# An encoder trunk on eight cores: feed-forward sums and products on VectorE alone, and a down projection one token block at a time

## The reference

```python
def swiglu(x, w_gate, w_up, w_down):
    return (jax.nn.silu(x @ w_gate) * (x @ w_up)) @ w_down
...
        h = swiglu(rms_norm(x, g[0]), ffn_w_gate[l, 0], ffn_w_up[l, 0], ffn_w_down[l, 0])
        x = x + HALF * rms_norm(h, g[1])
```

## Time and profile before

| | us |
|---|---|
| median of the 3 runs (2834.23, 2855.17, 2928.75) | 2855.17 |
| the profiled execution | 2832.33 |
| its slowest core, first to last instruction | 2830.8 |
| spans of its eight cores | 2819.8 to 2830.8 |
| PE busy on the slowest core | 2567.1 (91%) |
| DVE busy | 1661.7 (59%) |
| ACT busy | 1284.7 (45%) |
| POOL busy | 1160.9 (41%) |

### The profile page before, as it was taken

One profiled execution on the slowest core, in us unless ns is written; L12 is line 12 of the kernel. 1 busy time (PEld: TensorE's weight loads), 2 busy tenths in 40 slices (PEclk: granted clock), 3 DMA queues, 4 the chain that ended last, 5 costly groups with the idle time before them and its releaser, 6 DMA issues.

```text
span 2830.8 us, 39197 instructions; the slowest of 8 cores (2819.8 to 2830.8 us)
## 1 busy us (share of the span) xinstructions
PE 2567.1 (91%) x11634; PEld 1142.2 (40%) x11634; DVE 1661.7 (59%) x2166; ACT 1284.7 (45%) x2160; POOL 1160.9 (41%) x1337
## 2 busy tenths in 40 slices
PE   6899699988999799879969987997999996998997
PEld 2344244433454344334424433442445442443442
DVE  4752963455375964486197458616555669635643
ACT  5442443537777543344255344423117674433532
POOL 2742772115220674367167346710002106734751
PEclk8999899999999899989989999998999998999999
DMA  8455754748560355475475447553235504546767
GB/s 183 69 92 88 169 82 70 136 81 140 73 107 1 97 75 81 71 172 86 72 172 84 74 83 164 88 73 79 45 53 84 88 1 104 83 76 122 146 102 152
DMA packets 140349, 270.29 MB, mean 95 GB/s; under 512 B 16496, under 2 KB 35184, under 8 KB 140144
## 3 DMA queue, kind: packets, MB, share of 16 engines
q0 software_dynamic: 108432, 189.02, 44.6%
q1 hardware_dynamic: 31712, 78.77, 9.0%
HBM read 417.90 MB, written 34.60 MB: 160 GB/s over the span
## 4 chain that ended last, share of the span: by engine, by line
PE 76%; DVE 10%; issue 7%; ACT 3%; DMA 2%; POOL 1%; SPq 0%; DVEq 0%; ACTq 0%; POOLq 0%
PE ps L336 76%; DVE X L843 2%; DVE XH L799 2%; DVE X L842 1%; DMA X<-xT 1%; DVE XN L799 1%; DVE FE L1163 0%; DMA slotf_54<-wflat 0%; ACT L746 0%; DVE H L1014 0%; DVE ET_107 L1163 0%; DMA M_151<-memT 0%; DMA slotf_55<-wflat 0%; ACT r_65 L749 0%; POOL SW_0_82 L959 0%
## 5 line engine op out<-in xcount | busy, mean ns | idle before, releaser
L814 ACT ACTIVATE X<-ps,cf_sb 128x512 f32<-128x512 f32 x128 | 87.9, 687 | 429.5 <-PE ps L336 429.5
L336 PE MATMUL ps<-XH,SW_2_84 128*128 128x512 f16 x344 | 101.2, 422 | 69.4 <-DVE ER_88 L1000 16.0
L959 POOL TENSOR_TENSOR SW_0_82<-slotf_53 128x512 f16<-128x512 f16 x42 | 52.7, 1255 | 190.7 <-DVE X L843 190.2
L336 PE MATMUL ps<-XN,WQK 128*128 128x512 bf16 x512 | 124.0, 379 | 0.0
L336 PE MATMUL ps<-XH,SW_2_87 128*128 128x512 f16 x344 | 94.7, 400 | 24.5 <-DVE ER_89 L1000 12.8
L336 PE MATMUL ps<-TX_80,SW_1_86 128*128 128x512 f16 x344 | 90.7, 386 | 25.7 <-ACT ps L985 25.1
L985 ACT ACTIVATE ps<-ps 128x512 f32<-128x512 f32 x172 | 100.5, 584 | 28.9 <-PE ps L336 28.0
L843 DVE TENSOR_TENSOR X<-X 128x512 f32<-128x512 f32 x120 | 111.6, 958 | 0.0
L336 PE MATMUL ps<-TX_80,SW_1_83 128*128 128x512 f16 x344 | 92.0, 388 | 19.9 <-ACT ps L985 11.0
L792 ACT ACTIVATE XN<-X 128x512 bf16<-128x512 f32 x160 | 94.9, 628 | 20.0 <-DVE X L843 11.3
L336 PE MATMUL ps<-XH,slotf_52 128*128 128x512 f16 x360 | 96.6, 385 | 7.9 <-DVE XH L799 7.9
(11 more groups left out here) (528 smaller groups left out, 6542.8 us busy)
## 6 DMA issues: line engine op xcount, KB each, us to landing
xscr<-X SPq DMA_DIRECT2D x48, 512.0 KB, 9.1
X<-xscr SPq DMA_DIRECT2D x48, 512.0 KB, 7.6
slotf_52<-wflat POOLq DMA_DIRECT2D x62, 256.0 KB, 4.4
slotf_53<-wflat POOLq DMA_DIRECT2D x62, 256.0 KB, 5.0
slotf_54<-wflat POOLq DMA_DIRECT2D x62, 256.0 KB, 4.8
slotf_55<-wflat POOLq DMA_DIRECT2D x62, 256.0 KB, 5.1
slotf_56<-wflat POOLq DMA_DIRECT2D x62, 256.0 KB, 4.4
slotf_57<-wflat POOLq DMA_DIRECT2D x62, 256.0 KB, 5.4
```

The lines of the kernel that those rows point to most:

```text
L336: self.q["pe"].append((waits, (lambda e: e.matmul(out, lhsT=l_, rhs=r_, start=st, stop=sp, skip_group_check=grp)), inc))
L814: k.later({"act": lambda e: e.activation(out=oap, in_=P[bank][:, :], func=AF.Copy, scale=gcol)}, reads=[("P", bank)] + CONST, writes=okeys ...
L959: fn = lambda e: e.tensor_tensor(out=o_, in0=a, in1=b, op=op)
```

## The change

1. Line 959 (four a tile) and line 1024 (one a tile) may run on DVE alone; POOL is no longer a choice for them.
2. In the FFN, the addition to x in the post-norm (line 843) runs on DVE alone (`spread=False`). After the mixers and the attention it keeps its choice.
3. Every down stage goes one token block at a time: all 8 chunks of the first block, its `finish` (post-norm and, where there is a next sub-layer, the pre-norm of that block), then all 8 chunks of the second block. The panels are loaded for each block, 48 instead of 24 a half in halves 1 to 7. The pre-norm's squares are summed by DVE for the first block of a half and by PE for the second; before, DVE summed both in halves 1, 3, 4 and 5, and PE both in halves 2 and 6. Halves 7 and 8 have no pre-norm: their results are stored to `yT` (line 854).

```diff
--- before.py
+++ after.py
@@ -831,7 +831,7 @@
                     acc_add(sq, acc, sq, ak + sqk, sqk)
                     stat_later(self.st, self.psk, sq, sqk, True, False)
 
-            def apply(self, c):
+            def apply(self, c, spread=True):
                 tb = self.tb
                 lo, hi = tbr(tb)
                 st = self.st
@@ -842,12 +842,12 @@
                 mul = lambda e: e.tensor_tensor(out=hap, in0=hap, in1=R[st["r"]][:, :], op=ALU.mult)
                 add = lambda e: e.tensor_tensor(out=xap, in0=xap, in1=hap, op=ALU.add)
                 k.later({"dve": mul}, reads=hkeys + [self.rk], writes=hkeys, post=self.use, dyn=lambda: ([("R", st["r"])], []))
-                k.later({"dve": add, "pool": add}, reads=hkeys + [xk(c, tb)], writes=[xk(c, tb)])
-
-        def finish(pns, nxt, acc=True, by_chunk=False):
+                k.later({"dve": add, "pool": add} if spread else {"dve": add}, reads=hkeys + [xk(c, tb)], writes=[xk(c, tb)])
+
+        def finish(pns, nxt, acc=True, by_chunk=False, spread=True):
             order = [(pn, c) for c in range(8) for pn in pns] if by_chunk else [(pn, c) for pn in pns for c in range(8)]
             for pn, c in order:
-                pn.apply(c)
+                pn.apply(c, spread)
                 if nxt is None:
                     lo, hi = tbr(pn.tb)
                     yv = yT.rearrange("(c p) t -> p c t", p=128)
@@ -957,7 +957,7 @@
 
                 def ew(o_, a, b, op, rk, wk):
                     fn = lambda e: e.tensor_tensor(out=o_, in0=a, in1=b, op=op)
-                    k.later({"dve": fn, "pool": fn}, reads=rk, writes=wk, cost={"dve": 0.42, "pool": 1.5})
+                    k.later({"dve": fn}, reads=rk, writes=wk, cost={"dve": 0.42})
                 ew(s1, a21, a22, ALU.add, uk, q1)
                 ew(s2, s1, a11, ALU.subtract, q1 + gk, q2)
                 ew(a21, a11, a21, ALU.subtract, gk + uk, uk)
@@ -1022,7 +1022,7 @@
                     k.later({"act": lambda e: e.activation(out=e2, in_=e2, func=AF.Silu)}, reads=q2, writes=q2, func="silu")
                     hap, hkeys = H(j, (TB, 2 * TB))
                     fn = lambda e: e.tensor_tensor(out=hap, in0=e2, in1=e3, op=ALU.mult)
-                    k.later({"dve": fn, "pool": fn}, reads=q2 + q3, writes=hkeys, cost={"dve": 0.7, "pool": 1.4})
+                    k.later({"dve": fn}, reads=q2 + q3, writes=hkeys, cost={"dve": 0.7})
 
         def plain_tile(wg, wu, j, tb):
             lo, hi = tbr(tb)
@@ -1068,29 +1068,11 @@
                     if (l, f) == (0, 0):
                         mem_norm()
                     token_sums(1)
-                if nxt is None and hf == 1:
-                    for tb in tbs:
-                        tl = ((tb % 2) * TB, (tb % 2 + 1) * TB)
-                        pn = PostNorm(l, n_post, tb, True, hoap=ho_x(tb))
-                        for c in range(8):
-                            slots = [ws.acquire(("d", l, f, c, pc)) for pc in range(3)]
-                            b = k.bank()
-                            pairs = []
-                            for j in range(NJ):
-                                rap, rkeys = H(j, tl)
-                                sl = slots[j // 8]
-                                pairs.append((sl.w(j % 8), rap, rkeys + [sl.key]))
-                            k.mm(P[b][:, :], pairs, b)
-                            pn.evac(c, b)
-                            for sl in slots:
-                                ws.release(sl)
-                        finish([pn], nxt)
-                    continue
-                pn = {tb: PostNorm(l, n_post, tb, True, hoap=ho_x(tb)) for tb in tbs}
-                for c in range(8):
-                    slots = [ws.acquire(("d", l, f, c, pc)) for pc in range(3)]
-                    for tb in tbs:
-                        tl = ((tb % 2) * TB, (tb % 2 + 1) * TB)
+                for tb in tbs:
+                    tl = ((tb % 2) * TB, (tb % 2 + 1) * TB)
+                    pn = PostNorm(l, n_post, tb, True, hoap=ho_x(tb))
+                    for c in range(8):
+                        slots = [ws.acquire(("d", l, f, c, pc)) for pc in range(3)]
                         b = k.bank()
                         pairs = []
                         for j in range(NJ):
@@ -1098,12 +1080,13 @@
                             sl = slots[j // 8]
                             pairs.append((sl.w(j % 8), rap, rkeys + [sl.key]))
                         k.mm(P[b][:, :], pairs, b)
-                        pn[tb].evac(c, b)
-                    for sl in slots:
-                        ws.release(sl)
-                finish([pn[tb] for tb in tbs], nxt, hf == 0 or f == 1)
-                for c in range(8):
-                    x_reload(l, f, hf, c)
+                        pn.evac(c, b)
+                        for sl in slots:
+                            ws.release(sl)
+                    finish([pn], nxt, tb % 2 == 0, spread=False)
+                if nxt is not None or hf == 0:
+                    for c in range(8):
+                        x_reload(l, f, hf, c)
 
         def even_mixer(l, n_post, nxt):
             cpk = lambda sg, q: ("CP", sg, q)
```

## The result

The changed kernel takes 2674.74 us (median of 4 runs, 2661.38 to 2706.22), the kernel before beside it 2891.96 (median of 4 runs, 2834.23 to 2961.16). The ratio is **0.9387, with a 95% interval of 0.9249 to 0.9525**: faster. The profiled execution took 2661.38 us (predicted: 2660), its slowest core 2659.8, its cores 2649.5 to 2659.8, so 171 us less than the profiled execution before.

A forecast was written before the change was run, and what follows sets the result against it. PE was taken as the bound, losing time at stage starts behind the norms on DVE and ACT. Terms -119.6 - 14.3 - 32.6 - 15.6 - 4 + 14 = -172 from 2832.3 gave 2660 us; 80% range 2605 to 2735.

The forecast's parts named there:

- After FFN halves: Gate/up stages of halves 2, 4, 5 and 6: excess over the floor falls from 151.6 us together to 8 each, -119.6.
- Half 8: Its gate/up stage, with a post-norm alone ahead: excess falls from 19.3 us to 5, -14.3.
- Odd mixer: The first block's 15.6 us of norm now lie under the down stage: -15.6 us, between -8 and -18.
- Even mixer: In a 50 us stretch of PE's matmuls, 4 of 6.2 us lost are won back.
- After attention: Gate/up stages of halves 3 and 7: norm order unchanged, only prices fall; excess of 64.6 us together halves, -32.6.
- Panels twice: Second panel loads in halves 1 to 7: +4.6 us where half 7's stores join, 1.5 each in halves 1 to 6.
- Middle of a tile: Gate/up tiles: four sums and four result instructions take DVE 4.4 of 6.04 us, so the middle of the stage costs nothing.
- late sums in every tile: Rival: a weight sum reaches PE late in each gate/up tile; 172 tiles cost 34 us, 2694 us; 5%.
- memory-bound down stages: Rival: panels read at twice the rate arrive at 104 GB/s or less, making the kernel slower, 2889 us; 3%.
- late weights: Rival: every down stage waits like the end of half 8 or twice that, 18 to 50 us more, 2678 to 2710; 10%.
- The first rival: Three more sums a tile on an already full DVE cost 11 us a transition, 79 in seven stages: 2739 us; 7%.
- The stretching is not POOL's: Rival: DVE's prices stay as they are and only the halving by token blocks counts: 2742 us; 8%.

The follow-up runs named there:

- pair of reading and writing kernels: Changed kernel plus unused POOL work in each gate/up tile: six additions reading SBUF, 2774.6 to 2779.4 us; or twelve memsets only writing, 2844.71 us (fastest of three).
- the sums alone: Kernel before with line 959, line 1024 and the FFN's line 843 on DVE alone, down stages as before: 0.962 of before, fastest run 2747.40 us.
- `blocks only`: Changed kernel with lines 959, 1024 and 843 allowed on POOL again, down stages still one token block at a time: 0.950 of before, fastest run 2719.24 us.
- half of the memsets: Changed kernel with six unused memsets on POOL in each gate/up tile instead of twelve: 2661.33 and 2662.86 us, 0.935 of before.

## Why the prediction was right

The total, 2660 against 2661.38 for the profiled execution, is right by its main steps. That it is right to 1 us is luck, since errors of up to 10 us cancel in two pairs:

- **After FFN halves** (151.6 to 8 each): 8.2, 8.1, 11.6 and 8.6. Half 5, where four token sums also stand on DVE, is 3.6 over. Of the terms of the 8, DVE's is the better one: at the start of half 4 PE waits 2.1 us for ACT (4 were taken) and 1.7 for DVE (2); the eight matmuls stand at the 1.7 estimated, and some 2.6 us are in no wait of the profile.
- **Half 8** (to 5): 5.9. **Odd mixer** (-15.6): -15.4. **Even mixer** (-4): -4.2 on the slowest core, but some -7 on most of the others (407.6 to 409.4 us on the eight cores before, 399.9 to 404.4 after). **Half 1** (0, up to -10): -4.5, its down stage included, where the eight cores of one execution differ by 7 to 9. It makes up for the 4.5 that the stages after FFN halves won less than forecast.
- **After attention** (-16 each): -11.3 and -11.0. The step that failed is that "the order of the norms is unchanged; only prices fall": the planner gave POOL four additions that had all lain on DVE, and one a stage took 7.67 us behind a busy DVE. With them on DVE it is -15.8 and -14.5. The 149 us named as a sign for these stages was missed by 5.
- **Panels twice** (+14): half 7 +5.5 (+3.8 to +6.2 over the cores) instead of the 4.6 read from the earlier trace rows; halves 2 to 6 0 instead of 1.5 each. Too much here made up for too little after attention.
- **Middle of a tile** (nothing): right. In the changed kernel PE has no wait between 960 and 1043 us.

Of the rivals, late sums in every tile and memory-bound down stages did not come, nor did late weights beyond half 7, which the forecast had. The first rival, DVE as the bound at the transitions, came in small: DVE is without a gap in some 20 us after attention (with line 843 on DVE there), where seven additions fewer gave 1.4 us, and at the start of half 5, the stage that is 3.6 over, PE waits 4.6 us for weight sums. "The stretching is not POOL's" is refuted by the pair of reading and writing kernels, not only by the durations.

One argument was weaker than it looked. The 1.64 and 1.93 us of the earlier trace rows were read where POOL was busy; over the whole kernel before, line 843 of the FFN had a median of 681 ns and a mean of 958, as its rows from two views show, so at least half of its instructions were not stretched at all:

```profile
L843 DVE TENSOR_TENSOR X<-X x120: 674/681/3530, 274.1 to 2826.6; 128x512 f32<-128x512 f32 x120
...
L843 DVE TENSOR_TENSOR X<-X 128x512 f32<-128x512 f32 x120 | 111.6, 958 | 0.0
```

That fits the sums alone bringing 50 us after FFN halves, and not the 72 that I expected of them. The blocks alone bring 89, more than half: the first block's norm goes to a place where POOL has no sums, so that it loses its stretching with its place. The trace of `blocks only` shows that on line 799, first under half 3's down stage (1057 to 1134 us), where POOL only issues transfers, then at the start of half 4 (1134 to 1281 us), where it has sums again:

```profile
L799 DVE SCALAR_TENSOR_TENSOR XH<-X,cf_sb,r x8: 743/744/752, 1127.1 to 1131.8; 128x512 f16<-128x512 f32 x8
...
L799 DVE SCALAR_TENSOR_TENSOR XH<-X,cf_sb,r x8: 739/1188/1887, 1161.2 to 1169.7; 128x512 f16<-128x512 f32 x8
```

How many of the 89 us are this and how many the halving, no run separates.

## What to carry to other kernels

An engine that offers help on a shared path is to be priced by what it does to its neighbour's instructions: compare the median and the maximum of one line, in stages with and without the helper, and its mean before taking an extreme for the price. Then look for the reverse, the helper's own instruction that is held up behind a busy neighbour with a third engine waiting. And a norm that stands between two matmul stages can often go under the first of them by finishing half of the rows early; what the second load of the weights costs is read from the transfers' share where other traffic joins, not from the doubled bytes.

## What the runs showed that I had not expected

- A POOL addition of 128x512 in float32 takes 1.28 us, and 7.67 where DVE runs two-operand instructions without a gap; DVE's instructions meanwhile keep 0.69. With POOL reading in every tile it was a tile's first sum that rose, from 0.42 to 0.89. Either engine can be the one that waits. The Trainium skill, SBUF — State Buffer, Who interferes with whom, has this as well: it is the order of issue that decides which of the two is kept out. That POOL can be the one, the 7.67 us show; they last through a whole run of DVE's instructions, not through one of 0.69.
- Work on POOL that costs DVE nothing can still cost the kernel: at 6.0 of 6.04 us a tile POOL's queue let panels come late, and PE waited 130 us; with half of the memsets it waited 7.8.
- At 142 GB/s and share 0.95 of the transfer engines a down stage of matmuls lost nothing; at 158 over the stage, with stores joining late in it, it lost 5.5 us.
